# A two-block sequence model on one core: the order of turns and copies in the first attention, layers written out, state-space products grouped

## The chip, the cores and the metric

One core of one Trainium2 chip runs the whole program in one launch. The metric is the device time of an execution in microseconds. Three runs of the kernel before took 2785.29, 2787.04 and 2799.25 us; their median is 2787.04.

The engines are called by the names of the profile: PE is TensorE (matmuls, and turns of a tile, which are matmuls against an identity), PEld its weight loads, DVE VectorE, ACT ScalarE, POOL GpSimd, SP the queue that issues most DMAs.

## The reference

The input is x of 1024 rows and 1024 columns in float32. Two blocks follow each other.

The first block has two layers. Each layer is

```
h = rms_norm(x) * g;   p = h @ w_in            # split into c_q, c_kv, k_pe, z_a, u_f, z_f, g_a, g_f
q = rms_norm(c_q) @ w_uq;   k, v = rms_norm(c_kv) @ w_ukv (+ shared k_pe)
q, k = rms_norm per head (96 wide), rotated in the last 32 columns
o_a = softmax(q k^T / sqrt(96)) v              # 8 heads, 1024 x 1024 scores each, v 64 wide
y_a = (o_a * silu(z_a)) @ w_attn_proj
y_f = (real(fft2(u_f)) * silu(z_f)) @ w_fourier_proj
x = x + (sigmoid(g_a + b0) * y_a + sigmoid(g_f + b1) * y_f) @ w_out
```

The second block has one layer. An indexer scores keys for each query, the best 256 admissible keys are kept, and 8 heads attend to their shared 128-wide latent. Beside it runs a state-space branch: 32 groups of 16 channels, each with a diagonal complex state of 64, `x_t = A x_{t-1} + B u_t`, `y_t = Re(C x_t) + D u_t`, then GELU and a gated product. Both are gated, joined, projected and layer-normed.

## The kernel before

All five engines have a program of their own and meet at semaphores. PSUM has eight banks of 512 columns; for each bank b there is `full[b]`, raised by TensorE, and `free[b]`, raised by the engine that reads it out. `Banks` counts the uses of each bank at build time, so that each wait gets the right number. `Steps` does the same for an engine that waits for its own last result. The order of work on each engine is written by hand; there is no planner.

The two layers of the first block are one body in a hardware loop (`pe.Fori(0, L)` and its like on each engine). `enter` and `leave` of the two classes make the counts depend on the loop's register. The second block is straight code.

**First attention.** The work of a layer is 64 units: 8 heads times 8 tiles of 128 queries. On TensorE (line 596 on) unit u is: `scores(u + 1)` into a pair of banks (six matmuls of 512 columns, because each operand is split into a rounded part and a rest); if u is even, `pv_pair(u - 1)`, the product of the probabilities of two units with v (L588); `p_turn(u)`, the turn of the probabilities into banks 4 and 5 (L574); and in four units of each head `qk_turn` for the next head (L548, bank 7).

VectorE (line 1720 on) takes for unit u the negated row maximum of the scores (L1726), then copies the first half of the turned probabilities of unit u-1 out of bank 4 (L1733), and then, where there was a q/k turn, computes the rest `qk_rest` (L1709). Once a head it also copies the head's output (`head_out`).

ScalarE (line 1295 on) takes for unit u the exponential (L1300, with the row sum), then copies the second half of unit u-1 out of bank 5 (L1305), and then, where there was a q/k turn, rounds it (`qk_copy`, L1283). In the last head the q/k work is gone; instead ScalarE and VectorE round the normed h for the next stage (`round_h`, `in_place`, `rest_of_h`).

GpSimd prepares the normed and rotated q and k of the next head in a staging buffer, as soon as the turns of the last head have read it.

**State-space branch.** The 32 groups are worked in four calls f = 0 to 3 of 8 groups each, two groups to a pair k: group i = 0 has its states in partitions 0 to 63, i = 1 in 64 to 127. `s5_kernel(f)` turns the input powers (L766) and makes the short kernels with 64-row products of 16 and 112 columns (L778, L779). `s5_states(f)` makes the block states (L791). GpSimd rotates them, VectorE scans them (L2037), GpSimd rotates them back. `s5_outputs(f)` adds for each group one 128-row product (L808) and two 64-row products (L809, L810) in one bank. Between these calls TensorE computes gates (L749). Over the same stretch VectorE selects the top keys (L2023, L2024) and takes up the scans at fixed places between the selections. The second attention needs the finished selection, the queries' latents from TensorE (L912) and the layer norm's parameters, whose loads are issued after L912.

## Time and profile before

| what | us |
|---|---|
| median of three runs | 2787.04 |
| the profiled execution | 2788.53 |
| its span | 2786.7 |
| TensorE busy | 2603.2 |
| VectorE busy | 1328.1 |
| ScalarE busy | 826.5 |
| GpSimd busy | 348.1 |

The mean granted TensorE clock over the span is 0.976 of full speed. The first attentions lie at about 243 to 506 us (layer 0) and 1211 to 1474 us (layer 1) of the span, the state-space stage at about 2092 to 2457 us, and the second attention from there to the end. A busy time is the union of an engine's instructions; a sum over idle time of a line tells how long its engine stood before it, and the name behind the arrow what ended most of that.

### The profile page before, as it was taken

The numbers are of one execution on the slowest core, as the hardware profiler recorded it, in microseconds if no ns is written. First come the engines' busy times: TensorE is split into PE (matmuls) and PEld (weight loads), VectorE is DVE, ScalarE is ACT, GpSimd is POOL, SyncE is SP. The second block draws the span as 40 slices with busy tenths as digits, with TensorE's granted clock in tenths as the row PEclk, the third lists the DMA queues.
The fourth block names the chain that finished last, engine by engine and source line by source line (L and its number), as shares of the span: only waits on it lengthen the run. The fifth ranks groups of instructions, "written<-read, shape, count | busy, mean of one in ns | idle before, by whom it ended". The sixth has DMA issues, their size and how long they took to land.

```text
span 2786.7 us, 32034 instructions
## 1 busy us (share of the span) xinstructions
PE 2603.2 (93%) x12253; PEld 1807.7 (65%) x12253; DVE 1328.1 (48%) x2130; ACT 826.5 (30%) x1485; POOL 348.1 (12%) x463
## 2 busy tenths in 40 slices
PE   7998998899999999989988999999989999989998
PEld 5856776686666877567776766668547555445553
DVE  2353655321112233446553211132589989955763
ACT  3233455321112132335553211121251212133341
POOL 0012221000000000122300000000043853100000
PEclk9998999999999999989999999999999999999998
DMA  5110000211112121000002111130400011010000
GB/s 190 39 49 1 1 1 1 63 46 46 46 46 93 61 92 57 31 1 1 1 1 66 42 46 46 46 121 0 130 31 9 31 39 38 30 61 31 31 16 30
DMA packets 106738, 119.16 MB, mean 43 GB/s; under 512 B 21020, under 2 KB 77080, under 8 KB 106584
## 3 DMA queue, kind: packets, MB, share of 16 engines
q1 hardware_dynamic: 105432, 112.87, 13.1%
q10 hardware_dynamic: 1152, 4.19, 0.4%
q8 instruction: 101, 1.65, 0.2%
q14 instruction: 53, 0.43, 0.1%
HBM read 99.03 MB, written 16.84 MB: 42 GB/s over the span
## 4 chain that ended last, share of the span: by engine, by line
PE 78%; DVE 7%; ACT 6%; issue 6%; SPq 1%; POOL 1%; DMA 1%; ACTq 0%; DVEq 0%; POOLq 0%
PE PS L657 8%; PE PS L627 6%; PE PS L630 6%; PE PS L633 6%; PE PS L749 5%; PE PS L454 4%; PE PS L978 4%; DVE negm L1726 4%; PE PS L588 3%; PE PS L671 2%; PE PS L674 2%; PE PS L677 2%; PE PS L846 2%; PE PS L891 2%; PE PS L949 2%
## 5 line engine op out<-in xcount | busy, mean ns | idle before, releaser
L627 PE MATMUL PS<-hHi,R2bR 128*128 128x512 f32 x768 | 306.8, 399 | 15.7 <-ACT rows L1332 15.7
L630 PE MATMUL PS<-hLo,R2bR 128*128 128x512 f32 x768 | 300.6, 391 | 0.0
L633 PE MATMUL PS<-hHi,R2bR 128*128 128x512 f32 x768 | 300.5, 391 | 0.0
L1745 DVE TENSOR_TENSOR R2bR<-W,R2bR 128x1024 fp32r<-128x1024 f32 x48 | 57.5, 1222 | 309.9 <-ACT R2bR L1320 309.9
L1300 ACT ACTIVATE R2b<-PS,negm 128x1024 f32<-128x1024 f32 x128 | 142.7, 1115 | 209.4 <-DVE negm L1726 209.4
L588 PE MATMUL PS<-R2b,R 128*64 128x128 f32 x2048 | 130.8, 281 | 56.9 <-ACT R2b L1305 56.9
L1352 ACT ACTIVATE R3a<-PS,pT 128x512 f32<-128x512 f32 x64 | 42.3, 688 | 467.3 <-PE PS L633 467.3
L1726 DVE TENSOR_REDUCE negm<-PS 128x1 f32<-128x1024 f32 x128 | 155.9, 1218 | 45.8 <-PE PS L564 45.8
L627 PEld LDWEIGHTS PS<-hHi,R2bR 128*128 128x128 f32 x768 | 145.4, 189 | 49.2 <-ACT hHi L1291 16.1
L588 PEld LDWEIGHTS PS<-R2b,R 128*64 128x64 f32 x2048 | 116.9, 141 | 82.1 <-issue 80.1
L630 PEld LDWEIGHTS PS<-hLo,R2bR 128*128 128x128 f32 x768 | 145.5, 189 | 33.1 <-issue 3.3
L749 PE MATMUL PS<-hT,W 128*128 128x512 f32 x384 | 166.9, 595 | 0.0
L2178 POOL TENSOR_TENSOR R<-R,rsh 128x768 f32<-128x768 f32 x16 | 23.8, 1488 | 1130.6 <-DVE rsh L1683 838.8
L633 PEld LDWEIGHTS PS<-hHi,R2bR 128*128 128x128 f32 x768 | 145.2, 189 | 30.5
L574 PE MATMUL PS<-ident,R2b 128*128 128x128 f32 x1024 | 138.9, 279 | 2.0 <-ACT R2b L1300 1.1
L2023 DVE MAX8 ssc<-R2a 128x8 f32<-128x384 f32 (+4 forms) x160 | 132.4, 827 | 5.4
L749 PEld LDWEIGHTS PS<-hT,W 128*128 128x128 f32 x384 | 73.0, 191 | 91.2 <-issue 91.1
L574 PEld LDWEIGHTS PS<-ident,R2b 128*128 128x128 f32 x1024 | 115.6, 143 | 24.7 <-issue 12.7
L2024 DVE MATCH_REPLACE8 R2a<-ssc,R2a 128x384 f32<-128x384 f32 (+4 forms) x160 | 129.4, 809 | 0.0
L454 PE MATMUL PS<-W,hT 128*128 128x256 f32 (+1 forms) x512 | 122.0, 398 | 1.1 <-DMA W<-in_w_in 1.1
L1780 DVE TENSOR_TENSOR R3a<-R3a,PS 128x512 f32<-128x512 f32 x64 | 43.8, 684 | 162.7 <-PE PS L657 162.6
L978 PE MATMUL PS<-W,R 128*128 128x512 f32 x256 | 118.4, 608 | 0.8 <-DVE R L2071 0.8
(347 smaller groups left out, 4809.2 us busy)
## 6 DMA issues: line engine op xcount, KB each, us to landing
W<-in_w_in SPq DMA_DIRECT2D x10, 2048.0 KB, 8.2
W<-in_w_in SPq DMA_DIRECT2D x33, 512.0 KB, 5.1
xres<-R SPq DMA_DIRECT2D x3, 4096.0 KB, 18.2
W<-in_w_out SPq DMA_DIRECT2D x6, 2048.0 KB, 7.8
R<-xres SPq DMA_DIRECT2D x2, 4096.0 KB, 18.8
W<-in_c_dft_s SPq DMA_DIRECT2D x2, 2052.0 KB, 8.7
R<-in_x ACTq DMA_DIRECT2D x8, 512.0 KB, 8.1
W<-in_w_in SPq DMA_DIRECT2D x4, 1024.0 KB, 6.7
```

Of the source, the lines that this page charges most:

```text
L454: mm = pe.matmul(o[:, 0:hi - lo], hT[:, k, t * P:(t + 1) * P], wc[:, k, lo:hi], start=(k == 0), stop=(k == 7))
L574: mm = pe.transpose(o[:, k * P:(k + 1) * P], Pb[u % 2][:, c * P:(c + 1) * P], ident[:, :])
L588: mm = pe.matmul(PS[e * VD:(e + 1) * VD, 6, at_], v_tok[:, k, h, :], PT[e][:, k * P:(k + 1) * P], start=(k == 0), stop=(k == 7))
L627: mm = pe.matmul(o, wHi[c % 2][:, k, :], hHi[:, k, ns], start=(k == 0), stop=False)
L630: mm = pe.matmul(o, wHi[c % 2][:, k, :], hLo[:, k, ns], start=False, stop=False)
L633: mm = pe.matmul(o, wLo[c % 2][:, k, :], hHi[:, k, ns], start=False, stop=(k == 7))
L657: mm = pe.matmul(o, g[:, k0 + k, :], rhs[:, k, n * 512:(n + 1) * 512], start=(k == 0), stop=(k == 3))
L749: mm = pe.matmul(o, wz[:, k, m * P:(m + 1) * P], xT[:, k, n * 512:(n + 1) * 512], start=(k == 0), stop=(k == 7))
L978: mm = pe.matmul(o, mix[:, k, t * P:(t + 1) * P], wo[:, k, :], start=(k == 0), stop=(k == 7))
L1300: act.activation(Pb[u % 2], PS[:, b:b + 2, :].rearrange("p a c -> p (a c)"), ACT.Exp, bias=negm[:, u:u + 1], accum_out=rsum[:, u:u + 1]).t ...
L1726: dve.tensor_reduce(negm[:, u:u + 1], PS[:, b:b + 2, :].rearrange("p a c -> p (a c)"), AX.X, ALU.max, negate=True).then_inc(s_nm, 1)
L2023: st.link(dve.max(m8, sel[t]))
```

## The change

Five things change.

1. The layers are written out: every `Fori` becomes a Python loop, and `enter`, `leave` and the counts per layer go. SP no longer loads layer 0's parameters again in the middle of layer 1, and two waits for them go.
2. `QK_TURNS` names the units with a q/k turn: for head 1 units 1, 2, 3 and 5, for head h units 8(h-1)-1, +1, +3 and +5, so one to each odd unit. Before, they were in units 1 to 4 of a head. On TensorE the q/k turn now stands ahead of `p_turn(u)` of its unit.
3. The readers of banks 4 and 5 change. Where u is odd (the probabilities of an even unit u-1), VectorE copies both halves, and ScalarE none. Where u is even, VectorE copies the first half and ScalarE the second.
4. ScalarE does its copy ahead of the exponential of the unit.
5. In the state-space branch the 64-row products alternate between the two halves of the rows (i = 0, 1) one by one, in `s5_kernel` and `s5_outputs`, and in `s5_outputs` the eight 128-row products come first, all together.

```
+def qk_steps(h):
+    return [1, 2, 3, 5] if h == 1 else [NT * (h - 1) + n for n in (-1, 1, 3, 5)]
+QK_TURNS = {u: (h, i) for h in range(1, H) for i, u in enumerate(qk_steps(h))}
...
-            with pe.Fori(0, L) as l:
-                bk.enter(l)
+            for l in range(L):
...
                     if u >= 2 and u % 2 == 0:
                         pv_pair(u - 1)
+                    if u in QK_TURNS:
+                        qk_turn(*QK_TURNS[u])
                     if u < UNITS:
                         p_turn(u)
-                    if 1 <= u % NT <= 4 and u // NT + 1 < H:
-                        qk_turn(u // NT + 1, u % NT - 1)
...
-                    o = begin(2 + i)
-                    for k in range(HP):
-                        q, r_ = k, slice(NST * i, NST * i + NST)
-                        qq = f * HP + q
-                        for (lo, hi, cr, ci) in ((0, CH, CT[r_, 0, qq, :], CT[r_, 1, qq, :]),
-                                                 (CH, P, ca_re[p][r_, q, 0:CL - 1, :], ca_ni[p][r_, q, 0:CL - 1, :])):
-                            oo = o[0:CH, k * P + lo:k * P + hi]
-                            pe.matmul(oo, Bb[r_, 0, qq, :], cr, start=True, stop=False)
-                            mm = pe.matmul(oo, Bb[r_, 1, qq, :], ci, start=False, stop=True)
-                    mm.then_inc(full[2 + i], 1)
+                    begin(2 + i)
+                for k in range(HP):
+                    qq = f * HP + k
+                    for lo, hi in ((0, CH), (CH, P)):
+                        for j, (ct, ca) in enumerate(((CT[:, 0, qq, :], ca_re[p]), (CT[:, 1, qq, :], ca_ni[p]))):
+                            for i in range(2):
+                                r_ = slice(NST * i, NST * i + NST)
+                                c = ct[r_] if lo == 0 else ca[r_, k, 0:CL - 1, :]
+                                mm = pe.matmul(PS[0:CH, 2 + i, k * P + lo:k * P + hi], Bb[r_, j, qq, :], c,
+                                               start=(j == 0), stop=(j == 1))
...
-                        pe.matmul(og, UT[:, 2 * HP * f + g, :], TT[p][:, g, :], start=True, stop=False)
-                        pe.matmul(og, X[p][r_, 0, q, :], ca_re[p][r_, q, :, :], start=False, stop=False)
-                        mm = pe.matmul(og, X[p][r_, 1, q, :], ca_ni[p][r_, q, :, :], start=False, stop=True)
+                        pe.matmul(o[:, k * P:(k + 1) * P], UT[:, 2 * HP * f + g, :], TT[p][:, g, :],
+                                  start=(k == 0), stop=False)
+                for k in range(HP):
+                    for j, ca in enumerate((ca_re[p], ca_ni[p])):
+                        for i in range(2):
+                            r_ = slice(NST * i, NST * i + NST)
+                            mm = pe.matmul(PS[:, 6 + i, k * P:(k + 1) * P], X[p][r_, j, k, :], ca[r_, k, :, :],
+                                           start=False, stop=((k, j) == (HP - 1, 1)))
...
-                parameters(1 - l)
+                if l + 1 < L:
+                    parameters(l + 1)
...
                 for u in range(UNITS + 1):                       # ScalarE
+                    if u >= 1:
+                        bk.take(4)
+                        if u % 2 == 0:
+                            o = arrive(5)
+                            act.activation(PT[1][:, 512:1024], o, ACT.Copy).then_inc(free[5], 1)
+                        else:
+                            bk.take(5)
                     if u < UNITS:
...
                         act.activation(Pb[u % 2], PS[:, b:b + 2, :].rearrange("p a c -> p (a c)"), ACT.Exp,
                                        bias=negm[:, u:u + 1], accum_out=rsum[:, u:u + 1]).then_inc(free[b], 1)
-                    if u >= 1:
-                        o = arrive(5)
-                        bk.take(4)
-                        act.activation(PT[(u - 1) % 2][:, 512:1024], o, ACT.Copy).then_inc(free[5], 1)
...
                     if u >= 1:                                   # VectorE
-                        o = arrive(4)
-                        bk.take(5)
-                        dve.tensor_copy(PT[(u - 1) % 2][:, 0:512], o).then_inc(free[4], 1)
-                    if 2 <= u % NT <= 5 and u // NT + 1 < H:
-                        qk_rest(u // NT + 1, u % NT - 2)
+                        if u % 2 == 1:
+                            arrive(5)
+                            bk.take(4)
+                            dve.tensor_copy(PT[0][:, 0:512], PS[:, 4, :]).then_inc(free[4], 1)
+                            dve.tensor_copy(PT[0][:, 512:1024], PS[:, 5, :]).then_inc(free[5], 1)
+                        else:
+                            bk.take(5)
+                            o = arrive(4)
+                            dve.tensor_copy(PT[1][:, 0:512], o).then_inc(free[4], 1)
+                    if u - 1 in QK_TURNS:
+                        qk_rest(*QK_TURNS[u - 1])
...
-            dve.wait_ge(s_par, 96 * (L + 1))
```

## Rows read from the trace of the kernel before

**Rows 1.** The page's chain of work that ended last, by engine.
```profile
PE 78%; DVE 7%; ACT 6%; issue 6%; SPq 1%; POOL 1%; DMA 1%; ACTq 0%; DVEq 0%; POOLq 0%
```

**Rows 2.** Idle time before L588's instructions: who ended it, us, times.
```profile
  ACT R2b L1305: 56.9, 64
```

**Rows 3.** Stages: window and its length, busy PE, PEld, DVE, ACT, POOL, clock, DMA.
```profile
256.26:467.70 211.44, 191.20 (x1728) 162.27 (x1729) 127.29 (x155) 106.10 (x190) 53.42 (x66) 1.00 0.01 1
```

**Rows 4.** Timeline of PE in the first attention: start us, us, instruction, idle before.
```profile
264.37 1.97 PE L588 MATMUL PS<-R2b,R 128*64 128x128 f32 x32 [0.60 <-ACT R2b L1305]
...
272.48 1.97 PE L588 MATMUL PS<-R2b,R 128*64 128x128 f32 x32 [1.02 <-ACT R2b L1305]
274.38 1.09 PE L574 MATMUL PS<-ident,R2b 128*128 128x128 f32 x8
275.23 0.48 PE L564 MATMUL PS<-R3aR 96*128 96x512 f32 x1
...
278.74 0.40 PE L564 MATMUL PS<-R3aR,WR 96*128 96x512 f32 x1
280.00 1.97 PE L588 MATMUL PS<-R2b,R 128*64 128x128 f32 x32 [0.86 <-ACT R2b L1305]
...
286.71 0.39 PE L564 MATMUL PS<-R3aR,WR 96*128 96x512 f32 x1
287.53 1.97 PE L588 MATMUL PS<-R2b,R 128*64 128x128 f32 x32 [0.44 <-ACT R2b L1305]
```

**Rows 5.** Timeline: DVE, ACT in an even unit; a p turn and its copies.
```profile
261.29 1.21 DVE L1726 TENSOR_REDUCE negm<-PS 128x1 f32<-128x1024 f32 x1
...
262.53 1.11 ACT L1300 ACTIVATE R2b<-PS,negm 128x1024 f32<-128x1024 f32 x1 [1.88 <-DVE negm L1726]
...
263.64 0.59 ACT L1305 ACTIVATE R2b<-PS 128x512 f32<-128x512 f32 x1
...
499.57 1.09 PE L574 MATMUL PS<-ident,R2b 128*128 128x128 f32 x8
500.26 0.69 DVE L1733 COPY R2b<-PS 128x512 f32<-128x512 f32 x1 [2.19 <-PE PS L574]
500.70 0.60 ACT L1305 ACTIVATE R2b<-PS 128x512 f32<-128x512 f32 x1 [1.39 <-PE PS L574]
```

**Rows 6.** Timeline of ACT in the last head: the copy and what follows.
```profile
481.81 0.59 ACT L1305 ACTIVATE R2b<-PS 128x512 f32<-128x512 f32 x1
...
482.29 1.06 ACT L1291 ACTIVATE hHi<-hT 128x1024 fp32r<-128x1024 f32 x1
```

**Rows 7.** Timeline of PE at the start of layer 1.
```profile
987.41 0.47 PE L434 MATMUL PS<-ident,rows 128*128 128x128 f32 x1 [5.16 <-issue]
```

**Rows 8.** Timeline of PE: one call's first and last output products; kernel products; L912.
```profile
2202.58 0.46 PE L808 MATMUL PS<-R3a,R 128*128 128x128 f32 x2
...
2210.69 0.38 PE L810 MATMUL PS<-rtp,R3b 64*128 64x128 f32 x2
...
2093.33 0.35 PE L778 MATMUL PS<-R2b,rt 64*16 64x112 f32 x2
2093.52 0.35 PE L779 MATMUL PS<-R2a,rt 64*16 64x112 f32 x2
...
2451.71 7.24 PE L912 MATMUL PS<-R3a,u_mid 64*128 64x512 f32 x32 [0.74 <-ACT u_mid L1496]
```

**Rows 9.** Timeline of POOL and DVE in the state-space stage, and of DVE after it.
```profile
2202.59 0.95 POOL L2214 TENSOR_TENSOR R3b<-rt,kpe 128x448 f32<-128x448 f32 x1
...
2290.24 17.72 DVE L2037 TENSOR_TENSOR_SCAN R3b<-gk,R3b 128x128 f32<-128x128 f32 x16 [5.37 <-POOL R3b L2217]
...
2465.04 0.29 DVE L2121 CUSTOM_DVE_ANT_0 R3b<-PS,R2a 128x128 f32<-128x128 f32 x1 [7.67 <-DMA R3a<-in_ln_b]
```

**Rows 10.** The page: the span, and the queue that carries instructions.
```profile
span 2786.7 us, 32034 instructions
...
q8 instruction: 101, 1.65, 0.2%
```

More of the change, by code:

```diff
@@ L43 @@
 FIXED = [UNITS // 2, 0, UNITS // 2, 0, UNITS, UNITS, H, 4 * H]
-BANK_USES = [sum((n + 7 - b) // 8 for n in ROUND) + FIXED[b] for b in range(8)]
 CHUNKS = [(3, "c"), (1, "u"), (2, "up"), (1, "dft"), (1, "zf"), (1, "za")]
@@ L115, in __init__ @@
     def __init__(self, eng, sem):
-        self.eng, self.sem, self.n, self.layer, self.per = eng, sem, 0, None, 0
-    def enter(self, layer, per):
-        self.layer, self.per, self.start = layer, per, self.n
-    def leave(self, layers):
-        assert self.n - self.start == self.per, (self.n - self.start, self.per)
-        self.layer, self.n = None, self.start + layers * self.per
+        self.eng, self.sem, self.n = eng, sem, 0
     def done(self, ins):
@@ L129, in wait @@
     def wait(self):
-        self.eng.wait_ge(self.sem, self.n if self.layer is None else self.layer * self.per + self.n)
+        self.eng.wait_ge(self.sem, self.n)
     def link(self, ins):
@@ L1071, in _ @@
             parameters(0)
-            with sp.Fori(0, L) as l:
+            for l in range(L):
                 chunk(l, 0)
@@ L1185, in arrive @@
                 return PS[:, b, :]
-            with act.Fori(0, L) as l:
-                bk.enter(l)
-                st.enter(l, PER)
+            for l in range(L):
                 def x_std(t):
@@ L1571, in arrive @@
                 return PS[:, b, :]
-            with dve.Fori(0, L) as l:
-                bk.enter(l)
-                st.enter(l, PER)
+            for l in range(L):
                 o = arrive(0)
@@ L2160, in _ @@
             pool.wait_ge(s_const, 64)
-            with pool.Fori(0, L) as l:
-                bk.enter(l)
-                st.enter(l, 9 * H)
+            for l in range(L):
                 for n in ROUND[:7]:
```

32 lines of the change are left out of this document (8 added, 24 removed).

## The prediction

> **What bounds the kernel now.** I read the chain of waits first. TensorE (PE) is 78% of it, VectorE (DVE) 7%, ScalarE (ACT) 6% [rows 1]. So the gain has to come out of TensorE's time, or out of the waits between TensorE's pieces. The page has TensorE busy in nearly all of the span, but a busy share is an average. I therefore looked at the two stages that the change touches.
>
> First, the attention of the first block. The line of the value matmuls (L588) shows 56.9 us of idle time in 64 waits, all ended by ScalarE's copy at L1305 [rows 2]. That is one wait per pair of units, 32 pairs in each of two layers. In 211.44 us of that stage VectorE is busy for 127 us and ScalarE for 106 us, so neither is full [rows 3]: an order of work is late, not an engine.
>
> Second, the state-space stage of the second block. There VectorE selects top keys without a pause, except 5.37 us that it waits for GpSimd (POOL) and 7.67 us just before the second attention [rows 9]. Both limits matter below, because TensorE could run ahead of VectorE there.
>
> **Attention, as it is.** A pair of units without a q/k turn runs from 272.48 to 280.00, 7.52 us. TensorE's own pieces are: value matmuls 1.90, turn of the probabilities (p turn) 0.85, then from 275.23 scores, a p turn and scores again, whose last matmul starts at 278.74. Scores are 6 matmuls; with 0.8 for the p turn they are about 1.48 a group, 0.25 a matmul. So the own time ends at 278.99: 6.51 us, and then 1.0 us of waiting. The pair 280.00 to 287.53 has one q/k turn. Its own time is 286.71 + 0.25 - 280.00 = 6.96, so a q/k turn costs 0.45, and 0.57 is waited [rows 4]. Seven of the eight heads are made of such pairs, one q/k turn to a pair on average; they take 211.44 / 27 = 7.83 us each in the stretch of [rows 3].
>
> Why it waits: in an even unit u ScalarE does exp(u) first and then the copy of the second half of unit u-1. The maximum starts at 261.29, exp at 262.53, the copy at 263.64, and the value matmuls start at 264.37, 0.73 after the copy's start. The turn whose result is copied was done long before: a half is ready 0.69 us after the start of its p turn, the second half 1.13 us (499.57, 500.26, 500.70) [rows 4, 5].
>
> **Attention, changed.** I lay one pair out, with 0 at the start of the value matmuls of even unit u. TensorE: value matmuls to 1.90, p turn(u) to 2.75, scores(u+2) to 4.23, q/k turn to 4.68, p turn(u+1) to 5.48, scores(u+3) to 6.96. What must be ready:
> - VectorE, odd unit: max(u+1) from about 0.2 to 1.4; both halves of u are turned at 1.90 + 1.13 = 3.03; copies 3.03 to 4.40. The banks are wanted again at 4.68 and about 5.1, so they are free, with 0.2 us or more to spare. Then max(u+2) 4.45 to 5.65, copy of the first half of u+1 5.65 to 6.35, the q/k rest, also 512 columns out of PSUM (0.69), to 7.0. The next maximum can start at about 7.2.
> - ScalarE: exp(u+1) at 1.45; q/k copy at about 5.0; copy of the second half of u+1 at 4.68 + 1.13 = 5.81; value matmuls may start at 5.81 + 0.73 = 6.54, and TensorE comes there at 6.96. Spare: 0.4 us. Behind this copy stands exp(u+2), about 6.3 to 7.6 instead of 5.7 to 7.0. Its p turn is at 6.96 + 1.90 = 8.86, so the later exp costs nothing; without the 1.3 us of cover it would cost 0.6 a pair.
> - GpSimd makes the next head's q and k after the turns of the last one. The first q turn moves to the last unit of the head before, six units or more behind the turns that release the staging, so it stays covered.
> - The head's output (two copies of about 0.7) stands ahead of the double copy once a head; it makes the next maximum about 0.3 late, with 1.2 us of cover in exp.
>
> So a pair is TensorE's own 6.96. From 256.26 to 467.70 there are 27 pairs and 27 q/k turns before and after: 27 x 6.96 = 187.9 instead of 211.44 [rows 3, 4]. **Gain 23.5 a layer, 47.0 in two.**
>
> Last head: there ScalarE and VectorE drive in a ring (exp, copy, two roundings, rest, maximum), and TensorE idles. In odd units the copy leaves the ring, in even units it moves to a place ahead of exp where ScalarE is idle. Copy to next instruction is 0.48 [rows 6]; in four units 1.9. At the very end two copies on VectorE in a row give back about 0.6, and the last two value matmuls lose about 0.8 of wait: 2.0 a layer, **4 in all**.
>
> **Layers written out.** TensorE stands idle 5.16 us at the start of layer 1, and its end is put down to issue, no engine [rows 7]. The branch has to be taken there. Written out, what stays is a semaphore's way, below 1 us. **Gain 4.2**, once. The maximum: 5.2; the minimum 0. The register arithmetic ahead of waits goes too; no row of idle time prices it, so I bound it by 0 and 5 us and take 0. The 6 small parameter DMAs left out in the middle of layer 1 are behind nothing that TensorE waits for: 0. The removed wait for them at the end is for loads long landed: 0.
>
> **State-space products.** One call of the output products takes 2210.69 + 0.3 - 2202.58 = 8.45 us for 24 products of 2 instructions each [rows 8]. An instruction of 128 columns costs 0.107 (an eight-instruction p turn is 0.85), so the work is 48 x 0.107 = 5.1, and the rest are pauses at the changes from 128 rows to 64 and back, about 0.2 each, 16 of them. Grouped, there is one change each way. And pairs on the two halves of the rows can run side by side: the 32 instructions at L912, whose halves alternate, take 7.24 us, 0.226 for 512 columns, while 512 columns at the pitch of 0.107 for 128 would take 0.43 [rows 8]. So: 16 x 0.107 + 0.4 + 32 x 0.107/2 = 3.8. Saved 4.6 a call; if the halves don't overlap 2.9. In the kernel products, 112-column instructions cost 0.19 for two [rows 8]; 32 of them a call, 3.04, become 1.5; the 16-column ones stay. Saved 1.2 a call (I take 1.2; lowest 0).
> What is on the path: the second call of the output products also waits for GpSimd's states, and GpSimd goes on to its next work only at 2202.59 [rows 9]; so the second call can't start earlier than now, and of the two savings one counts, 4.6. With two kernel calls, 2.4, the second half of the stage starts 7.0 earlier. GpSimd's rotations hang on it, so VectorE's 5.37 wait is gone and its selection ends at 2457.4 - 5.4 = 2452.0. TensorE's side gains two more output calls, 9.2: 16.2 in all, and would allow 2465.04 - 16.2 = 2448.8 [rows 9]. What is late next is VectorE: start at 2452.1 instead of 2465.04. **Gain 13.0.** If the halves don't overlap, TensorE's side gives 3 x 2.9 = 8.7 and VectorE 2.9 + 7.67 = 10.6: gain 8.7.
>
> **Sum.** 47.0 + 4 + 4.2 + 13.0 = 68.2. The profiled execution took 2788.5 (span 2786.7), 1.5 above the median of the three runs shown, 2787.0. 2787.0 - 68.2 = 2719.
>
> **Rivals.**
> - A wait takes the place of the one removed in the attention. For it: the spares are only 0.2 to 0.4 us, and VectorE carries two copies in a row. Against: its durations in a pair sum to 2 x 1.22 + 3 x 0.69 + 0.69 = 5.2 of 6.96. If half of the gain per pair stays as a wait (0.45 x 54 = 24): 2743. The Trainium skill ("TensorEngine Tiling (Array Packing)", PSUM Bottleneck) advises to use both ScalarE and VectorE for emptying PSUM, which speaks against VectorE taking both halves; by that rule the result would be this one, and [rows 3], with VectorE busy for 60% of the stage, bears it out little so far. 15%.
> - No overlap of the halves of rows: 13.0 becomes 8.7, time 2723. For it: K = 64 products here have never been seen alternating one by one. Against: L912. 12%.
> - The change doesn't do what it says for the state-space part: VectorE's selection hides all but the 7.67, time 2724. It needs GpSimd's chain to stay where it is. 6%.
> - Slower: the written-out program fetches its instructions from straight code. The fetches show in queue q8: 101 packets [rows 10]. If a fetch held TensorE up, the only price in sight is 4.2 us [rows 7]; half of it on each of 101 is 212 us less the 64 gained elsewhere: 2787 + 148 = 2935. It decides from 68/101 = 0.7 us a fetch on. Against: 1.65 MB over the 32034 instructions executed is 52 bytes for each, so the loop's second pass seems to have been fetched as well, and no stall but the branch's shows in it. 3%.
> - The forecast 64%.
>
> **How the numbers follow.** The forecast, both small state-space rivals and most of the first are within 2703 to 2745: down by 5 for the register arithmetic, some more for a head's edges and for pauses between pieces, up by the attention rival. A measurement of this kernel tells about 0.5% (14 us) from no change. All cases but the fetch are faster by more than that, unless the attention gains nothing at all: faster 95%, same 2%, slower 3%.
>
> **What would show it.** Value matmuls every 6.9 to 7.0 us through seven heads, with no idle time ended by L1305's copy; VectorE's double copy starting 1.1 us after the p turn; no 5 us gap between the layers; output products in under 4 us a call, kernel products shorter by a quarter; the wait of 5.37 gone, and VectorE the one that the second attention waits for. Wrong: a pair above 7.3 us with an idle time ended by VectorE's copy; output calls of 5.5 us; new idle time put down to issue in straight code.

## The result, and the profile after

The changed kernel took 2721.82 us (median of 4 runs, 2720.41 to 2722.85), the kernel before 2786.82 on the same chip (2785.29 to 2799.25). The ratio of the means is 0.9757 [0.9728, 0.9785]; the medians are 65 us apart. The forecast was 2719. So the size was right, in part by luck: two parts of the sum came out lower than forecast, and time that no part of the sum stood for made up for it.

Lines have moved: the value matmuls are L575 (L588 before), p turns L561, scores L551, q/k turns L535, the exponential L1295, ScalarE's copy L1288, its q/k copy L1271, VectorE's maximum L1712, its double copy L1720 and L1721, its copy in even units L1725, the q/k rest L1695, the output products L793 (128 rows) and L799 (64 rows), the kernel products L764.

The page of the kernel after, where it answers to [rows 10], [rows 1] and [rows 2]: the span, the instruction queue, the chain by engine, and the two groups of the attention whose idle time changed most (busy, mean ns, then idle time and what ended it).

```profile
span 2719.1 us, 30167 instructions
...
q8 instruction: 98, 1.61, 0.2%
...
PE 84%; DVE 8%; ACT 4%; issue 1%; POOL 1%; SPq 1%; DMA 1%; DVEq 0%; POOLq 0%; ACTq 0%
...
L1295 ACT ACTIVATE R2b<-PS,negm 128x1024 f32<-128x1024 f32 x128 | 142.4, 1112 | 78.6 <-DVE negm L1712 78.6
...
L575 PE MATMUL PS<-R2b,R 128*64 128x128 f32 x2048 | 128.3, 279 | 6.5 <-DVE R2b L1725 3.2
```

TensorE's share of the chain rose from 78% to 84%, "issue" fell from 6% to 1%. That fall belongs to writing the layers out ("issue" is 1% in a_unroll below, 6% in a_ssm), which by itself gave 2.4 us: a share of the chain is not a gain. The 56.9 us of idle time ended by ScalarE's copy [rows 2] are gone; what is left before the value matmuls is 6.5. The view of ScalarE's copy line, L1288, says the same from the other side (who waited for it, us, times):

```profile
  PE PS L575: 1.6, 2
```

The stretch that answers to [rows 3], from the first value matmuls of a layer to those of the last head's first unit, went from 211.44 us to 189.83. VectorE carries 141.40 us in it instead of 127.29, ScalarE 94.23 instead of 106.10 (columns as in [rows 3]):

```profile
254.17:444.00 189.83, 189.13 (x1729) 161.41 (x1728) 141.40 (x180) 94.23 (x163) 53.45 (x66) 1.00 0.01 1
```

One pair of units in TensorE's timeline, the answer to [rows 4], and ahead of it the layer's first pair, which is different (start, us, instruction, idle before):

```profile
256.06 0.64 PE L535 MATMUL PS<-ident,R 128*96 128x128 f32 x4
...
259.65 0.61 PE L535 MATMUL PS<-ident,R 128*96 128x128 f32 x4 [0.70 <-DVE WR L1695]
...
262.45 1.97 PE L575 MATMUL PS<-R2b,R 128*64 128x128 f32 x32
...
269.45 1.97 PE L575 MATMUL PS<-R2b,R 128*64 128x128 f32 x32
...
273.66 0.60 PE L535 MATMUL PS<-ident,R 128*96 128x128 f32 x4
274.10 1.04 PE L561 MATMUL PS<-ident,R2b 128*128 128x128 f32 x8
...
276.45 0.77 PE L575 MATMUL PS<-R2b,R 128*64 128x128 f32 x10
```

From 262.45 on the value matmuls come every 7.00 us with no idle time marked before them. The first pair takes 8.28: it holds two q/k turns, in units 2 and 3, and the second of them waits 0.70 for VectorE's q/k rest.

VectorE and then ScalarE in the same pair:

```profile
272.47 0.69 DVE L1720 COPY R2b<-PS 128x512 f32<-128x512 f32 x1 [1.70 <-PE PS L561]
273.08 0.68 DVE L1721 COPY R2b<-PS 128x512 f32<-128x512 f32 x1
...
275.00 0.68 DVE L1725 COPY R2b<-PS 128x512 f32<-128x512 f32 x1
275.60 0.68 DVE L1695 TENSOR_TENSOR WR<-PS,R3aR 96x512 fp32r<-96x512 f32 x1
```

```profile
274.30 0.59 ACT L1271 ACTIVATE R3aR<-PS 96x512 fp32r<-96x512 f32 x1 [2.28 <-PE PS L535]
275.17 0.60 ACT L1288 ACTIVATE R2b<-PS 128x512 f32<-128x512 f32 x1 [0.28 <-PE PS L561]
275.67 1.11 ACT L1295 ACTIVATE R2b<-PS,negm 128x1024 f32<-128x1024 f32 x1
```

Counted from the value matmuls at 269.45, the layout made by hand can be laid over these rows: double copy at 3.02 (predicted 3.03), q/k turn 4.21 (4.23), even unit's copy on VectorE 5.55 (5.65), ScalarE's copy 5.72 (5.81), exp 6.22 (about 6.3), next pair 7.00 (6.96). The copy at 5.72 would let the value matmuls go at 6.45; TensorE comes at 7.00.

The start of layer 1, the answer to [rows 7]; the 5.16 us put down to issue are 1.03 us, ended by VectorE:

```profile
956.52 0.30 PE L421 MATMUL PS<-ident,rows 128*128 128x128 f32 x1 [1.03 <-DVE R L1800]
```

The state-space stage, the answer to [rows 8]: the first two output calls; the wait before the last states; the gated product; then the 16 DMA issues of SP that copy the short kernels to their places.

```profile
2138.15 3.75 PE L793 MATMUL PS<-R3a,R 128*128 128x128 f32 x16 [2.87 <-issue]
...
2146.78 2.02 PE L793 MATMUL PS<-R3a,R 128*128 128x128 f32 x16 [1.74 <-POOL R3b L2202]
2148.73 0.49 PE L799 MATMUL PS<-R2b,R3b 64*128 64x128 f32 x4
...
2150.72 5.85 PE L735 MATMUL PS<-hT,W 128*128 128x512 f32 x13
...
2221.04 0.88 PE L778 MATMUL PS<-R,R3b 128*64 128x128 f32 x5 [6.77 <-ACT R3b L1429]
...
2271.39 58.16 PE L882 MATMUL PS<-R,W 128*128 128x512 f32 x128 [4.74 <-issue]
```

```profile
2183.60 10.87 SPq L1137 DMA_DIRECT2D R3a<-R3a  x16
```

The second call is 2150.72 - 2146.78 = 3.94 us instead of 8.45. The first still takes 6.89, from 2138.15 to 2145.04: its 128-row products run at a granted clock of 0.50. It costs nothing, because TensorE then waits 1.74 us for GpSimd. In all TensorE now stands 2.87 and 1.74 us around the first call, and 6.77 instead of 4.55 before the states. VectorE's scans and its start of the second attention, the answers to [rows 9], and TensorE's first score product there:

```profile
2229.35 17.72 DVE L2026 TENSOR_TENSOR_SCAN R3b<-gk,R3b 128x128 f32<-128x128 f32 x16 [0.28 <-POOL R3b L2202]
...
2395.27 1.21 DVE L2013 MATCH_REPLACE8 R2b<-ssc,R2b 128x1024 f32<-128x1024 f32 x1
2398.85 0.29 DVE L2110 CUSTOM_DVE_ANT_0 R3b<-PS,R2a 128x128 f32<-128x128 f32 x1 [2.38 <-DMA R3a<-in_ln_b]
```

```profile
2395.28 0.68 PE L918 MATMUL PS<-R2b,R 128*128 128x128 f32 x4 [2.38 <-ACT R L1490]
```

The wait of 5.37 is 0.28. VectorE is through with the selection at 2396.48 and still waits 2.38, so its selection isn't what is late. The load that its row names, and the time from its issue to its landing:

```profile
2393.31 0.43 SPq L1090 DMA_DIRECT2D R3a<-in_ln_b  x1
...
DMA to landing us min/median/max: 5.3/5.3/5.3
```

### The profile page after: what moved, and what is told of

It is laid out like the page before. It is cut to its first block, busy times and chain, and to the rows that moved or that the text cites. A ratio compares the mean times of both kernels' runs of the same rounds, so it can differ in the third digit from the quotient of the medians.

```text
span 2719.1 us, 30167 instructions
## 1 busy us (share of the span) xinstructions
PE 2574.2 (95%) x12253; PEld 1785.7 (66%) x12253; DVE 1364.7 (50%) x2194; ACT 796.1 (29%) x1420; POOL 348.1 (13%) x463
## 4 chain that ended last, share of the span: by engine, by line
PE 84%; DVE 8%; ACT 4%; issue 1%; POOL 1%; SPq 1%; DMA 1%; DVEq 0%; POOLq 0%; ACTq 0%
PE PS L644 8%; PE PS L614 6%; PE PS L617 6%; PE PS L620 6%; PE PS L551 6%; PE PS L441 4%; PE PS L575 4%; PE PS L561 4%; PE PS L969 4%; PE PS L735 4%; PE PS L882 2%; PE PS L658 2%; PE PS L661 2%; PE PS L664 2%; PE PS L940 2%; PE PS L486 2%
## 5 line engine op out<-in xcount | busy, mean ns | idle before, releaser
L1712 DVE TENSOR_REDUCE negm<-PS 128x1 f32<-128x1024 f32 x128 | 156.5, 1223 | 28.3 <-PE PS L551 23.4
L1295 ACT ACTIVATE R2b<-PS,negm 128x1024 f32<-128x1024 f32 x128 | 142.4, 1112 | 78.6 <-DVE negm L1712 78.6
L561 PE MATMUL PS<-ident,R2b 128*128 128x128 f32 x1024 | 139.0, 279 | 7.3 <-ACT R2b L1295 5.6
L575 PE MATMUL PS<-R2b,R 128*64 128x128 f32 x2048 | 128.3, 279 | 6.5 <-DVE R2b L1725 3.2
L575 PEld LDWEIGHTS PS<-R2b,R 128*64 128x64 f32 x2048 | 112.7, 139 | 29.1 <-issue 22.3
L561 PEld LDWEIGHTS PS<-ident,R2b 128*128 128x128 f32 x1024 | 114.3, 142 | 22.5 <-issue 13.2
```

The source lines that it names most:

```text
L561: mm = pe.transpose(o[:, k * P:(k + 1) * P], Pb[u % 2][:, c * P:(c + 1) * P], ident[:, :])
L575: mm = pe.matmul(PS[e * VD:(e + 1) * VD, 6, at_], v_tok[:, k, h, :], PT[e][:, k * P:(k + 1) * P], start=(k == 0), stop=(k == 7))
L1295: act.activation(Pb[u % 2], PS[:, b:b + 2, :].rearrange("p a c -> p (a c)"), ACT.Exp, bias=negm[:, u:u + 1], accum_out=rsum[:, u:u + 1]).t ...
L1712: dve.tensor_reduce(negm[:, u:u + 1], PS[:, b:b + 2, :].rearrange("p a c -> p (a c)"), AX.X, ALU.max, negate=True).then_inc(s_nm, 1)
```

## The experiments

Twelve kernels ran. One table of their traces serves all of them, in us. The ratio is that of the means, to runs of the kernel before on the same chip, whose median was 2784.89 for the four with a_, 2784.65 for those with b_ and 2785.97 for those with c_ and d_. Beside the kernels with b_, three of the seven runs of the kernel before took 2797 us or more, which lowers their ratios by about 0.002; so the kernels are compared by their own times and stages. "Stretch" is that of [rows 3]: 27 pairs of layer 0. "Last head" goes from its end to the layer's last value matmuls. "State space" goes from the first kernel turn of that stage (2092.22 in the kernel before, 2035.74 after) to the first score product of the second attention.

| kernel | median | ratio to before [95%] | stretch | last head | state space |
|---|---|---|---|---|---|
| before | 2786.82 | | 211.44 | 35.18 | 369.11 |
| after | 2721.82 | 0.9757 [0.9728, 0.9785] | 189.83 | 33.09 | 359.54 |
| a_unroll | 2782.49 | 0.9989 [0.998, 0.9999] | 213.24 | 35.26 | 370.62 |
| a_attn | 2728.61 | 0.9795 [0.9779, 0.9812] | 189.82 | 33.09 | 370.47 |
| a_ssm | 2773.81 | 0.996 [0.9946, 0.9974] | 211.35 | 35.22 | 359.71 |
| a_noalt | 2727.11 | 0.9791 [0.9772, 0.9811] | 189.84 | 33.07 | 363.74 |
| b_split | 2735.01 | 0.9801 [0.9749, 0.9854] | 194.54 | 35.18 | 359.84 |
| b_evenfirst | 2718.58 | 0.9743 [0.9691, 0.9794] | 188.99 | 33.75 | 359.70 |
| b_expfirst | 2756.19 | 0.9877 [0.9825, 0.993] | 205.10 | 35.36 | 359.70 |
| b_sel | 2720.97 | 0.9752 [0.9711, 0.9792] | 189.83 | 33.08 | 359.88 |
| c_head1 | 2717.91 | 0.9752 [0.9736, 0.9769] | 188.56 | 33.06 | 359.65 |
| c_ring | 2708.68 | 0.9723 [0.9707, 0.974] | 189.83 | 27.03 | 359.43 |
| d_warm | 2724.62 | 0.9781 [0.9765, 0.9798] | 189.83 | 33.07 | 362.40 |
| d_all | 2709.43 | 0.9728 [0.9712, 0.9744] | 188.56 | 27.03 | 362.04 |

The three columns of stages repeat to about 0.3 us between kernels in which a stage is the same, with one exception: the state-space stage with the old products took 369.11 us in the kernel before and 370.5 in the two kernels with the layers written out. The medians repeat less well. From the first q/k turn of a layer to its first value matmuls, for instance, the fourteen kernels took 20.65 to 23.15 us, whatever was changed in them. Differences of a few us are read from the stages.

### The three parts of the change, one by one

**a_unroll**: the layers written out, and nothing else.

```
-            with pe.Fori(0, L) as l:
-                bk.enter(l)
+            for l in range(L):
...
-                parameters(1 - l)
+                if l + 1 < L:
+                    parameters(l + 1)
...
-            dve.wait_ge(s_par, 96 * (L + 1))
```

> Only the layers are written out; attention and state-space products as before. Theory (a stall at the taken branch alone): the 5.16 us gap ahead of layer 1 becomes about 1 us, the pairs of units keep their 8.11 / 8.11 / 7.52 / 7.52 us, total 4 to 6 us less, near 2782. Rival (register arithmetic ahead of every wait costs time all over the layers): pairs get shorter by 0.05 us or more each and the total falls by 10 us or more. Rival (fetches of straight code stall engines): longer than before.

**a_attn**: the changed kernel, with the state-space products in their old order (the edits in `s5_kernel` and `s5_outputs` undone).

> Layers written out and the attention's new order, state-space products as before. Theory (each part stands alone, gains add): pairs of 7.00 us, no idle time ended by ScalarE's half copy, total 46 to 52 us below the kernel with the layers written out alone, near 2732. Rival (the parts hide one another, since the second block starts from the same point whatever comes before it): the sum of parts differs from the whole by more than 5 us.

**a_ssm**: the kernel before, loops and all, with those two edits alone.

> The kernel before with the state-space products grouped, nothing else. Theory (the selection on VectorE and the loads after L912 cap the gain): output products under 5 us a call, the 5.37 us wait of VectorE gone, total 9 to 12 us less, near 2777. Rival (VectorE or GpSimd hides nearly all of it): under 4 us less. Rival (all of TensorE's saving counts): 16 us or more less.

Writing out gave 2.4 us (2784.89 to 2782.49, both on that chip), not 4.2, and less than the 4 to 6 expected. The gap went as forecast; TensorE at the start of layer 1 in a_unroll:

```profile
979.71 0.30 PE L421 MATMUL PS<-ident,rows 128*128 128x128 f32 x1 [1.03 <-DVE R L1786]
```

What came back is in the attention: its stretch grew by 1.8 us a layer. The pairs with two q/k turns took 8.25 us instead of 8.11, the pairs without 7.52 as before. In such a pair the engines go round in a ring: ScalarE's q/k copy, VectorE's rest, the maximum, exp, copy, q/k copy. One step of it is longer. From the start of the q/k copy to the start of the rest it was 260.68 - 260.06 = 0.62 us in the kernel before; in a_unroll ScalarE's copy starts at 255.77 and the rest at

```profile
256.46 0.69 DVE L1687 TENSOR_TENSOR WR<-PS,R3aR 96x512 fp32r<-96x512 f32 x1 [1.28 <-ACT R3aR L1266]
```

which is 0.69: 0.07 more in each unit with a q/k turn, 0.14 a pair. The gap and the two stretches alone come to 4.1 - 3.6 = 0.5; the other 2 us lie in places that also differ between kernels where nothing in them was changed, and can't be put down to writing out. The start of layer 0's attention, for one, took 23.14 us before and 21.36 here, but 23.09 in a_noalt and 23.12 in d_warm, which are written out too. The hop itself is clear: in the two kernels with loops it is 0.62 in every unit where VectorE waits for the copy, in a_unroll 0.69. What makes that hop longer with constant counts than with counts from a register stayed open; in the changed kernel it is hidden: TensorE is busy 189.13 of the stretch's 189.83 us, so the ring no longer sets the pace.

So against its true starting point the attention part is worth more than the comparison with the kernel before shows: 213.24 - 189.82 = 23.4 us a layer. a_attn against a_unroll is 53.9 us, a little more than the 46 to 52 expected: 46.8 in the two stretches, 4.3 in the last heads, and 2.8 that I can't place. The state-space part gave 11.1 us alone (a_ssm) and, on top of the others, 2728.61 - 2721.82 = 6.8 by the medians, which were taken beside different runs of the kernel before (2784.89 and 2786.82). In its own stage it gave 369.11 - 359.71 = 9.4 alone and 370.47 - 359.54 = 10.9 on top: about 10 us in both surroundings.

### Which of the edits in the attention frees the pair

Theory: what held the value matmuls was that in even units ScalarE's copy stood behind exp. Rival: what matters is that VectorE takes both halves in odd units and unloads ScalarE.

**b_expfirst**: the changed kernel, with exp ahead of the copy in even units; VectorE's double copy stays (the lines are shortened).

```
 for u in range(UNITS + 1):                       # ScalarE
+    if u < UNITS:      # exp(u)
+        act.activation(Pb[u % 2], ..., ACT.Exp, ...)
     if u >= 1: ...     # even u: the copy of bank 5
-    if u < UNITS:      # exp(u)
-        act.activation(Pb[u % 2], ..., ACT.Exp, ...)
```

> The kernel after, but ScalarE does exp ahead of its copy in even units, as before the change; VectorE still copies both halves in odd units. Theory (the place of the copy behind exp is what made the value matmuls wait): the wait is back, 0.5 us or more ahead of the value matmuls, pairs of 7.5 us or more, total 25 us or more above after. Rival (the q/k turns and the double copy made the gain): pairs stay below 7.1 us.

**b_split**: each engine copies one half in each unit, ScalarE's copy always ahead of exp. Only ScalarE's side is shown; on VectorE the double copy becomes the copy of bank 4 alone.

```
-                        if u % 2 == 0:
-                            o = arrive(5)
-                            act.activation(PT[1][:, 512:1024], o, ACT.Copy).then_inc(free[5], 1)
-                        else:
-                            bk.take(5)
+                        o = arrive(5)
+                        act.activation(PT[(u - 1) % 2][:, 512:1024], o, ACT.Copy).then_inc(free[5], 1)
```

> The kernel after, but in every unit VectorE copies the first half and ScalarE the second, ScalarE's copy always ahead of the exponential. Theory (VectorE's double copy is needed, because in odd units ScalarE's exp would stand behind a half that is turned only 3.0 us into the pair): in odd units exp starts about 2 us later, its p turn waits, a pair takes 7.3 to 7.9 us instead of 7.00, total 16 to 50 us more. Rival (only the order copy before exp matters, not who copies): pairs stay at 7.00.

**b_evenfirst**: each engine copies one half in each unit; ScalarE's copy is ahead of exp in even units and behind it in odd ones. Again only ScalarE's side is shown, shortened.

```
+                    if u >= 1 and u % 2 == 0:
+                        half_copy()
                     if u < UNITS:
                         ...                      # exp(u)
+                    if u % 2 == 1:
+                        half_copy()
```

> The kernel after, but VectorE copies one half in every unit and ScalarE the other; ScalarE's copy is ahead of exp in even units and behind it in odd ones. Theory (TensorE is the bound once no half is late, and ScalarE has room): 7.00 us a pair, the last head 2 us a layer longer because the copy is back in its ring. Rival (the double copy on VectorE is what buys the time): pairs above 7.2 us.

b_expfirst is 34 us slower than the changed kernel: its pairs after the first take 7.52, 7.51, 7.51 and 7.72 us in turn. ScalarE's exp and copy of one even unit, and the value matmuls that wait for the copy:

```profile
275.27 1.11 ACT L1288 ACTIVATE R2b<-PS,negm 128x1024 f32<-128x1024 f32 x1 [0.23 <-DVE negm L1712]
...
276.38 0.59 ACT L1294 ACTIVATE R2b<-PS 128x512 f32<-128x512 f32 x1
```

```profile
277.11 1.10 PE L575 MATMUL PS<-R2b,R 128*64 128x128 f32 x16 [0.44 <-ACT R2b L1294]
```

The copy starts 1.11 us after exp, and the value matmuls 0.73 after the copy: the chain of [rows 5], back again though VectorE takes two copies. The order alone is worth 205.10 - 189.83 = 15.3 us of the 23.4 a layer, with the other edits in place. The rest, 213.24 to 205.10, came with three edits together: one q/k turn to a pair instead of two and none, the q/k turn ahead of the p turn, and the double copy. No run takes these three apart.

b_evenfirst says how little the double copy matters once the order is right: with it undone, the pairs are again 7.00 us, the first one even 7.44 instead of 8.28.

```profile
254.69:443.68 188.99, 188.99 (x1729) 161.48 (x1728) 125.87 (x153) 110.10 (x190) 53.44 (x66) 1.00 0.01 1
```

VectorE has 125.87 us of work there and ScalarE 110.10, and TensorE's 188.99 are without a gap. Its median is 3.2 us below the changed kernel's, but the intervals lie over each other, and the stages explain under 1 us of it; that it is faster isn't shown. That it is not slower is. The 2 us a layer that the copy was expected to cost in the last head were 0.7 in layer 0 (33.75 against 33.09) and none in layer 1. The Trainium skill ("TensorEngine Tiling (Array Packing)", PSUM Bottleneck) advises to use both engines for emptying PSUM. Here dividing the copies evenly or giving VectorE the pair made no difference once the order was right.

b_split shows where a copy ahead of exp does harm, though less than expected (7.3 to 7.9 us a pair): it came out between its theory and its rival. In odd units TensorE's p turn comes soon after and needs exp. ScalarE in one pair: exp waits there behind the copy, and the p turn behind exp, at 275.31 against the q/k turn's 274.75. In the changed kernel this step is 0.44 (273.66 to 274.10), here 0.56, and the turn itself is 0.06 longer:

```profile
273.56 0.60 ACT L1287 ACTIVATE R2b<-PS 128x512 f32<-128x512 f32 x1 [2.61 <-PE PS L561]
274.06 1.11 ACT L1292 ACTIVATE R2b<-PS,negm 128x1024 f32<-128x1024 f32 x1
```

```profile
274.75 0.60 PE L535 MATMUL PS<-ident,R 128*96 128x128 f32 x4
275.31 1.09 PE L561 MATMUL PS<-ident,R2b 128*128 128x128 f32 x8
```

The pair is 7.19: 0.19 x 25 = 4.7 us a layer (the first pair is 0.7 shorter than in the changed kernel, the last of the stretch 0.6 longer), and the last head is 2.1 longer; in two layers 13.6, and the medians are 13.2 apart. So the rule is by unit: the copy goes first where the value matmuls are next on TensorE, exp first where the p turn is.

### Do the two halves of the rows run side by side?

**a_noalt**: the changed kernel; the 128-row products stay together, but the 64-row products go one half after the other, and the kernel products are as before.

```
-                for k in range(HP):
-                    for j, ca in enumerate((ca_re[p], ca_ni[p])):
-                        for i in range(2):
+                for i in range(2):
+                    for k in range(HP):
+                        for j, ca in enumerate((ca_re[p], ca_ni[p])):
```

> The kernel after, but the 64-row output products go one half of the rows after the other (the 128-row products still first, all together), and the kernel products in the order of before. Theory (the halves overlap only when they alternate): a call's 64-row output products take 3.4 us or more instead of 1.8, kernel products 3.55 instead of about 2.0. Rival (the saving is only the fewer changes between 128 and 64 rows): 64-row products take 1.8 us still. Time of the whole: 1 to 4 us more than after.

The 64-row products of one call in a_noalt, its first and last group, and the next call:

```profile
2138.66 0.49 PE L798 MATMUL PS<-R2b,R3b 64*128 64x128 f32 x2
...
2141.77 0.38 PE L798 MATMUL PS<-R2a,R3b 64*128 64x128 f32 x2
2145.32 0.98 PE L792 MATMUL PS<-R3a,R 128*128 128x128 f32 x3 [3.17 <-issue]
```

The wait before the next call hides the end of the last of them. With 0.3 for it, as the prediction has it, they take 2142.07 - 2138.66 = 3.4 us, 0.107 for each of 32. Alternating, the same 32 end where the next work starts: 2150.72 - 2148.73 = 1.99. A call is 5.4 against 3.94. The halves do run side by side, at 1.7 times the rate. Of the 8.45 us of a call before, grouping saves 3.1 and alternating 1.4. In the whole, a_noalt's stage is 4.2 us longer than the changed kernel's; its median is 5.3 us longer, where 1 to 4 was expected. The Trainium skill says that tiles in different row groups run in parallel and that a change of the tiling mode drains the array ("TensorEngine Tiling (Array Packing)", Key Properties). This trace agrees with the first, 3.4 against 1.99 us, and adds that the order of issue decides: one half after the other gained nothing. The 3.1 us that went when 16 changes in a call became two fit the second; no run shows the drain by itself.

### What the second attention waits for

**b_sel**: the changed kernel with two rounds less in the selection of the last tile. It leaves out part of the selection.

```
-            select(7, range(0, TOPK // 8 - len(LATE)))
+            select(7, range(0, TOPK // 8 - len(LATE) - 2))
```

> The kernel after without two of the rounds of top-key selection of the last tile (that part of the selection is left out), 4.9 us less work on VectorE just before the second attention. Theory (TensorE's side, the loads behind L912, is what the second attention waits for): the start of the attention doesn't move, total within 1 us of after, VectorE's idle time before L2110 grows from 2.4 to about 7.3 us. Rival (VectorE's selection is the bound, as predicted): 4 to 5 us less.

VectorE's last step of the selection and its start of the second attention; then the load that the row names, and its time to landing:

```profile
2389.41 1.21 DVE L2013 MATCH_REPLACE8 R2b<-ssc,R2b 128x1024 f32<-128x1024 f32 x1
2397.43 0.29 DVE L2110 CUSTOM_DVE_ANT_0 R3b<-PS,R2a 128x128 f32<-128x128 f32 x1 [6.81 <-DMA R3a<-in_ln_b]
```

```profile
2391.96 0.43 SPq L1090 DMA_DIRECT2D R3a<-in_ln_b  x1
...
DMA to landing us min/median/max: 5.2/5.2/5.2
```

Against the stage's start VectorE was through 4.2 us earlier, and it waited 6.81 instead of 2.38; the stage is 359.88 us against 359.54. So the selection isn't what the second attention waits for. The row's name is right: the layer norm's second parameter lands at 2391.96 + 5.2 = 2397.2, and VectorE starts 0.24 us after it. It is 0.24 in the changed kernel too (2393.31 + 5.3, then 2398.85) and 0.24 or 0.25 in all fourteen kernels, while the distance to TensorE's first score product moves between 3.27 and 3.71. In the kernel, VectorE waits for both parameters (`dve.wait_ge(s2_ln, 32)`), and SP issues their loads only when TensorE is through with L903 (L912 before): the first is issued 7.3 us after the start of that line in both kernels. So TensorE's side decides, but through a load. Issued earlier, it would let VectorE start with the end of its selection or with TensorE's scores, up to about 2.4 us sooner in the changed kernel. That is an estimate from the wait of 2.38; it wasn't tried.

### The rests that the traces point to

**c_head1**: in head 1 a q/k turn moves from unit 2 to unit 0.

```
-    return [1, 2, 3, 5] if h == 1 else ...
+    return [0, 1, 3, 5] if h == 1 else ...
```

> The kernel after with head 1's q/k turns in units 0, 1, 3, 5 instead of 1, 2, 3, 5. Theory (the two turns next to each other cost the pair of 8.28 us its 1.28 us, and unit 0 has idle time on TensorE): second pair 7.0 to 7.2 us, and the first value matmuls not later: 1 to 2.6 us less in all. Rival (the first turn delays unit 0's own turn by as much): no change.

**c_ring**: in the last head the rounding of h (`in_place` on ScalarE, `rest_of_h` on VectorE) starts one unit later.

```
-                        if 2 <= u % NT <= 5:
-                            in_place(u % NT - 2)
+                        if 3 <= u % NT <= 6:
+                            in_place(u % NT - 3)
...
-                    if 1 <= u % NT <= 4 and u // NT + 1 == H:
-                        rest_of_h(u % NT - 1)
+                    if 2 <= u % NT <= 5 and u // NT + 1 == H:
+                        rest_of_h(u % NT - 2)
```

> The kernel after; in the last head VectorE's rest of h and ScalarE's rounding in place each come one unit later, so that the maximum never waits for a rounding of the same unit. Theory (the ring exp, roundings, rest, maximum sets the pace of the last head): its units take about 4 us instead of 5.5, 4 to 8 us a layer less, 8 to 16 in all. Rival (ScalarE's own work of about 4 us a unit and TensorE's 3.5 leave little): under 3 us in all.

c_head1 makes the first pair 7.00 us like the others: the stretch is 1.27 shorter, 2.5 in two layers, and its median 3.9 below the changed kernel's, which by the intervals can't be told from none. Part of it may only have moved, since the turn now stands ahead of the stretch; the starts of the two attentions were 22.08 and 23.01 us against 21.61 and 21.09, which is within their scatter. c_ring makes the last head 6.1 us shorter, 12.1 in two layers, and the median 13.1: 2708.68. The last head of the changed kernel and of c_ring, TensorE's two longest waits of the first and what stands in their place:

```profile
457.81 1.73 PE L561 MATMUL PS<-ident,R2b 128*128 128x128 f32 x8 [1.73 <-ACT R2b L1295]
...
468.86 1.09 PE L561 MATMUL PS<-ident,R2b 128*128 128x128 f32 x8 [1.79 <-ACT R2b L1295]
```

```profile
456.70 1.97 PE L575 MATMUL PS<-R2b,R 128*64 128x128 f32 x32 [0.61 <-DVE R2b L1725]
...
463.93 1.97 PE L575 MATMUL PS<-R2b,R 128*64 128x128 f32 x32 [0.58 <-DVE R2b L1725]
```

In the changed kernel VectorE computes the rest of a piece of h that ScalarE has only just rounded, and its maximum, the next exp and the p turn stand behind it. One unit later the piece is ready, and the ring no longer sets the last head's pace: TensorE's two waits for exp are gone, and its value matmuls come after 7.24 us instead of 11.00 and 8.59.

**d_warm**: 12 matmuls that nobody reads, ahead of the gated product, so that TensorE doesn't stand idle before it. **d_all**: c_head1, c_ring and d_warm together.

```
+            pe.wait_ge(free[0], bk.count(0))
+            for i in range(12):
+                pe.matmul(PS[:, 0, :], wg[:, i % 4, 0:P], xT[:, i % 4, 0:512], start=True, stop=True)
```

> The kernel after with 12 matmuls into a free bank, whose results nobody reads, while TensorE waits for the copies ahead of the gated product (L882). Theory (the first matmuls there run at the 1.2 GHz level after 4.7 us of idle time, which costs 2.9 us): L882 takes 55.1 us instead of 58.0, the second attention starts 2.4 to 2.9 us earlier. Rival (VectorE's selection is the bound): L882 is shorter but the total doesn't move.

> The last three put together. Theory (they are in different stages and add up): 11 to 20 us below after, near 2706. Rival (what is gained before the second attention is partly hidden by VectorE's selection): less than the sum of the three by 1 us or more.

In the changed kernel TensorE stands 4.74 us before the gated product and then works at half clock for 5.61 us. The granted clock (the column after POOL) in the two parts of it, and in d_warm in the filler and in the product:

```profile
2271.39:2277.00 5.61, 5.61 (x7) 2.50 (x8) 5.40 (x10) 0.00 (x0) 0.00 (x0) 0.50 0.27 43
2277.00:2329.39 52.39, 52.39 (x123) 22.99 (x121) 50.81 (x69) 11.59 (x16) 17.79 (x14) 1.00 0.00 0
```

```profile
2265.24:2275.55 10.31, 10.31 (x27) 4.57 (x26) 9.96 (x16) 4.87 (x6) 0.00 (x0) 1.00 0.68 203
2275.55:2330.48 54.93, 54.93 (x129) 24.32 (x128) 53.28 (x73) 11.59 (x16) 17.80 (x14) 1.00 0.00 0
```

The filler did what it was for: the product took 54.93 us instead of 58.00. But it was twice too long. 12 matmuls are 24 instructions of 0.43 us, 10.3 us in a hole of 4.74. From the start of the 32 turns ahead of the product to the product itself it went from 8.42 to 13.83 us, 5.4 lost for 3.1 won, and the stage is 2.9 us longer where 2.4 to 2.9 less was expected. A filler of 5 instead of 12 wasn't tried. d_all is where this leaves it, 2709.43: by the stages, what c_head1 adds to c_ring, the filler takes away. c_ring has the lowest median, 2708.68 us, 0.9723 [0.9707, 0.974] of the kernel before; c_ring with c_head1 alone wasn't run.

## Why the prediction was right, point by point

The profiled executions differ by 2786.7 - 2719.1 = 67.6 us of span; 68.2 were predicted.

- **Attention pairs: predicted 47.0, measured 43.2.** The mechanism was right, and the pair is 7.00 where TensorE's own pieces were summed to 6.96. The term that was mis-sized is "27 x 6.96": 25 pairs of 7.00 or close are 1.0 us more than that in a layer, the first pair of 8.28 is 1.3 more, the last of 6.56 is 0.4 less; together 189.8. The first pair was overlooked: head 1 has its q/k turns in units 1, 2, 3 and 5, so one pair has two, and VectorE's rest, behind two copies, isn't done in time. The prediction counted 27 turns on 27 pairs and checked one pair of the ordinary kind. c_head1 confirms the price.
- **Last head: predicted 4 in two layers, measured 2.1 + 3.0.** Right in size. Called a ring in the prediction, and c_ring shows how much was still in it: 12 us that a shift by one unit removes.
- **Gap between the layers: predicted 4.2, measured 4.1.** What stayed is 1.03 us, where "below 1 us" was taken. But the written-out layers as a whole gave 2.4 (a_unroll): 0.07 us a hop came in elsewhere, 3.6 in two layers, and about 2 us of scatter went the other way. "The register arithmetic ahead of waits goes too: 0 to 5 us" had the wrong lower end; it may cost. In the changed kernel no cost of it shows, since the ring is covered.
- **State space: predicted 13.0, measured 9.7 (2465.04 - 2092.22 = 372.82, 2398.85 - 2035.74 = 363.11).** The prices of the calls were right: an output call 3.94 (3.8 predicted) at full clock, two kernel calls with their turns 9.2 to 6.4, 2.8 saved where 2.4 was taken (the 16-column products pair up too). The error is in what lies on the path; the term mis-sized is the 16.2 for TensorE's side, which measured 9.6. Its first part, 7.0 up to the second half of the stage, is one output call, 4.6, and the two kernel calls behind it, 2.4. Of the second output call 3.8 counted: it starts 111.04 us after the stage's first turn, before 110.36, because it waits for GpSimd, as the prediction says. The two kernel calls saved 2.85, but 2.2 of it went into the wait before the states, 4.55 to 6.77: the way to them leads over SP's 16 DMA issues in a row, which take 10.61 us before and 10.87 after, and GpSimd's work behind them. So up to the states it was 3.8 + 2.85 - 2.2 = 4.4 and not 7.0. The last two output calls gained 7.6 (17.60 to 9.99) of 9.2, and the gated product, which the prediction didn't look at, gave 2.6 back: 3.0 in its own time, 55.0 to 58.0, at the half clock that d_warm removes, less 0.4 before it.
- **"What is late next is VectorE": wrong.** VectorE's selection ended 4.4 us earlier against the stage's start (5.4 predicted). TensorE's L903 came 9.6 earlier (16.2 predicted), and with it the load of the layer norm's parameters, whose landing is the later of the two; b_sel shows it. The prediction took this load as a fixed part of TensorE's side and didn't price it.
- **Not forecast:** 2.2 us at the two starts of the attention (23.14 to 21.61 in layer 0) and 1.6 from the second attention's start to the end. No edit can be named for either: the starts scatter from 20.65 to 23.15 us over the fourteen kernels, and from the first score product of the second attention to the end it is 325.4 us in the kernel before and 323.8 in the changed one, but 325.6 in a_noalt.

The four parts measured 43.2 + 5.1 + 4.1 + 9.7 = 62.1. Attention pairs and state space fell short by 3.8 and 3.3; the starts, the end and 1.7 us of small rests brought 5.5. So the forecast hit closer than its parts did, and that is luck: the four parts as measured would have given 2787.0 - 62.1 = 2724.9, still inside the stated range.

Of the rivals, the wait in the attention didn't come: the spare that was counted as 0.4 us is 0.55 in the trace, and the double copy waits for nothing but its p turn. That the row halves don't overlap is refuted by a_noalt. That VectorE's selection hides the gain is refuted by b_sel. The fetch of straight code costs nothing visible: q8 has 98 packets instead of 101, and "issue" is 1% of the chain.

## What to carry to other kernels

Where an engine serves two chains in turn, decide the order unit by unit, by what the bottleneck engine needs next; here that alone was worth 15 of 23 us a layer, and once the order was right it made no difference who does the copy. When a call gets shorter, ask for each copy of it which wait follows, and count the saving only where TensorE itself came last. When a wait names a DMA, add its time to landing to its issue: if the engine starts the same short time after it in every kernel (here 0.24 us), the name is right, and the next question is what held the issue back.

## What the runs showed of the hardware

- Two chains of 64-row float32 products of 128 columns, one on each half of the rows, run side by side when they alternate product by product (two instructions each): 1.99 us for 32 instructions. One half after the other took 3.4 (a_noalt).
- From the start of ScalarE's q/k copy to VectorE's instruction that waits for it was 0.62 us with counts taken from a loop register and 0.69 with constants. The cause stayed open.
- After idle times of 2.87 and 4.74 us TensorE went on at half clock: 16 instructions at L793 took 3.75 us at a granted 0.50, which is 1.2 GHz, instead of 2.02, and the gated product ran 5.61 us at 0.50. After 1.74 and 0.77 us it stayed at 1.00. After 3.51 us in the kernel before the same product ran at full clock (55.17 us), but there the 32 turns just ahead had already run at a mean of 0.68 and taken 5.35 us instead of 3.68. So part of what is saved ahead of a wait can be paid back in clock.
- A load of 512 KB issued on SP behind another of its kind (the layer norm's second parameter) landed 5.0 to 5.4 us after its issue in the fourteen kernels, and VectorE, which waited for it, started 0.24 or 0.25 us later.
